# Expert lists made in pairs, and additions that skip places without a token

## The reference

```python
def hierarchical_moe(h, w_coarse, w_fine, w_up, w_down):
    coarse = softmax(t @ w_coarse)                   # 4 groups, the best one is taken
    fine = (t @ w_fine) of that group                # 4 experts, the best two are taken
    gates = softmax(top 2) * group probability       # zero for the other 14 experts
    gu = einsum('nd,edf->nef', t, w_up)              # 16 experts, 1024 -> 2 x 256
    act = silu(g_part) * u_part * gates
    out = einsum('nef,efd->nd', act, w_down)         # 256 -> 1024, summed over the experts
```

## Time and profile before

| | us |
|---|---|
| median of 3 runs (lowest, highest) | 625.59 (621.91, 627.24) |
| the profiled execution | 628.41 |
| its span | 626.7 |
| TensorE busy | 551.8 |
| VectorE busy | 375.3 |
| ScalarE busy | 262.8 |
| GpSimd busy | 191.5 |

### The profile page before, as it was taken

How to read it: one execution, slowest core, us unless ns; L and a number is a source line. 1 busy time by engine, 2 the same in 40 slices (tenths; PEclk the granted TensorE clock), 3 DMA queues, 4 the chain that set the end, 5 groups by cost and what they waited for, 6 DMA issues and landing times.

```text
span 626.7 us, 7175 instructions
## 1 busy us (share of the span) xinstructions
PE 551.8 (88%) x2589; PEld 432.6 (69%) x2589; DVE 375.3 (60%) x615; ACT 262.8 (42%) x421; POOL 191.5 (31%) x354
## 2 busy tenths in 40 slices
PE   1699799999979899989999789935799999999982
PEld 1488687887667677677888678835668677676750
DVE  3885176683983884956666632365865766665530
ACT  6415035435433545364223311131463666665631
POOL 2549333089469269000000000002021341313111
PEclk9999799988989989999999889965897999999997
DMA  8524520220220210113364561597479799999954
GB/s 302 107 69 110 160 66 2 68 67 2 68 67 2 67 51 1 52 51 100 98 208 158 208 253 68 200 396 276 126 262 347 243 376 340 372 341 371 345 96 69
DMA packets 69220, 102.82 MB, mean 164 GB/s; under 512 B 10528, under 2 KB 42304, under 8 KB 69184
## 3 DMA queue, kind: packets, MB, share of 16 engines
q1 hardware_dynamic: 63184, 80.84, 37.6%
q0 software_dynamic: 4608, 16.78, 10.7%
q10 hardware_dynamic: 1392, 4.74, 1.9%
HBM read 88.71 MB, written 12.58 MB: 162 GB/s over the span
## 4 chain that ended last, share of the span: by engine, by line
PE 61%; DVE 15%; DMA 7%; ACT 7%; POOL 4%; issue 3%; SPq 1%; ACTq 0%; POOLq 0%; DVEq 0%
PE pj L1477 8%; PE pj L1479 8%; PE pj L1478 8%; PE m L1794 7%; DMA arena_front<-in_w_expert_up_dram 4%; PE pj L1774 4%; PE pj L1775 4%; PE pj L1776 4%; PE sc L1554 2%; PE tp L1762 2%; ACT arena_back L755 1%; SPq L481 1%; DMA arena_front<-h_rows,idx_all 1%; DVE arena_back L1190 1%; ACT arena_back L764 1%
## 5 line engine op out<-in xcount | busy, mean ns | idle before, releaser
L1477 PE MATMUL pj<-h_high,split 128*128 128x512 f32 x192 | 81.3, 424 | 2.7 <-DVE h_low L963 1.5
L1478 PE MATMUL pj<-h_low,split 128*128 128x512 f32 x192 | 78.4, 409 | 0.0
L1479 PE MATMUL pj<-h_high,split 128*128 128x512 f32 x192 | 78.2, 407 | 0.0
L1411 DVE TENSOR_TENSOR up_low<-arena_front,up_high 128x2048 fp32r<-128x2048 f32 x26 | 59.2, 2290 | 21.9 <-ACT up_high L827 21.9
L1794 PE MATMUL m<-arena_back 128*128 128x512 f32 x128 | 58.3, 598 | 2.8 <-ACT arena_back L839 2.8
L605 POOL DMA_INDIRECT out_dram<-arena_back,idx_all x16 | 29.8, 1866 | 101.2 <-DMA out_dram<-arena_back,idx_all 87.4
L1774 PE MATMUL pj<-up_high,xt_high 128*128 128x512 f32 x128 | 56.1, 438 | 5.3 <-DVE up_low L1411 3.7
L519 POOL TENSOR_TENSOR rstd<-ssq,half_col 128x1 f32<-128x1 f32 x8 | 6.4, 796 | 166.2 <-DVE ssq L940 166.2
L827 ACT ACTIVATE up_high<-arena_front 128x2048 fp32r<-128x2048 f32 x26 | 49.5, 1916 | 6.6 <-DMA arena_front<-in_w_expert_up_dram 5.7
L1775 PE MATMUL pj<-up_low,xt_high 128*128 128x512 f32 x128 | 50.7, 396 | 0.0
L1776 PE MATMUL pj<-up_high,xt_low 128*128 128x512 f32 x128 | 50.7, 396 | 0.0
(11 more groups left out here) (316 smaller groups left out, 1241.4 us busy)
## 6 DMA issues: line engine op xcount, KB each, us to landing
arena_front<-in_w_expert_up_dram SPq DMA_DIRECT2D x13, 2048.0 KB, 15.9
arena_back<-in_w_expert_down_dram SPq DMA_DIRECT2D x16, 1024.0 KB, 12.8
arena_front<-in_w_in_dram SPq DMA_DIRECT2D x13, 1024.0 KB, 5.6
arena_back<-in_w_expert_up_dram SPq DMA_DIRECT2D x3, 2048.0 KB, 17.3
arena_front<-in_w_out_dram SPq DMA_DIRECT2D x4, 1024.0 KB, 5.3
arena_back<-in_x_dram SPq DMA_DIRECT2D x4, 512.0 KB, 5.9
arena_front<-in_w_ssm_glu_gate_dram SPq DMA_DIRECT2D x8, 256.0 KB, 2.8
arena_front<-in_w_ssm_glu_val_dram SPq DMA_DIRECT2D x8, 256.0 KB, 3.6
```

What stands on the lines that cost most here:

```text
L1411: tt(up_low[e % NU][:, half(h)], ring[e % NU][:, half(h)], up_high[e % 2][:, half(h)].bitcast(F32), ALU.subtract).then_inc(up_low_done, 1)
L1477: pe.matmul(dst, sh, mh, start=first and i == 0, stop=False)
L1478: pe.matmul(dst, sh, ml, start=False, stop=False)
L1479: ins = pe.matmul(dst, sl, mh, start=False, stop=last and i == len(terms) - 1)
```

## The change

The lists of the experts 8 to 15 become four sets of two. TensorE makes a pair behind the up product in steps 1 to 4. VectorE chooses the pair at the start of the same step and reads it at the start of the next. All sets but the second are in bank `sc[0]`, each at its own columns.

The fourth column of `tg` becomes the token's number for a routed token and the number plus 512 for another. VectorE reads it into a new tile, `idx_own`. The addition takes its rows from `idx_own` with a bound of 511: an index above the bound is left out, and is no error. Gathers go by `idx_all` as before, so a place without a routed token is still gathered, multiplied and scaled (by zero).

```diff
-    LISTS = [0, 2, NE // 2, NE]
+    LISTS = [0, 2] + list(range(NE // 2, NE + 1, 2))
...
+        idx_own = sb("idx_own", [P, NE], U32)
...
-                g.indirect_dma_start(out_rows, bass.IndirectOffsetOnAxis(idx_all[:, e:e + 1], 0), y_out[e % 2], None,
-                                     compute_op=ALU.add).then_inc(y_added, 16)
+                g.indirect_dma_start(out_rows, bass.IndirectOffsetOnAxis(idx_own[:, e:e + 1], 0), y_out[e % 2], None,
+                                     compute_op=ALU.add, bounds_check=SEQ - 1, oob_is_err=False).then_inc(y_added, 16)
...
-            for n in (0, 3):
-                mark(v.tensor_copy(tg[:, :, :, n], bc(tok_id[:, :].rearrange("p (o t) -> p o t", o=1), [P, NE, TT])))
+            mark(v.tensor_copy(tg[:, :, :, 0], bc(tok_id[:, :].rearrange("p (o t) -> p o t", o=1), [P, NE, TT])))
...
-            mark(ts(r(7), r(6), -1.0, 1.0, ALU.mult, ALU.add))
+            link(ts(r(7), r(6), -1.0, 1.0, ALU.mult, ALU.add))
+            mark(stt(tg[:, :, :, 3], ev(r(7)), float(SEQ), bc(tok_id[:].rearrange("p (o t) -> p o t", o=1), [P, NE, TT]),
+                     ALU.mult, ALU.add))
...
                 v.tensor_copy(idx_all[:, lo:hi], got[:, :, 0])
+                v.tensor_copy(idx_own[:, lo:hi], got[:, :, 3])
                 v.tensor_reduce(gate_all[:, lo:hi], got[:, :, 1:3], AX_X, ALU.add).then_inc(idx_done, 1)
...
             for e in range(NE):
-                if e == 3:
-                    fill_lists(2)
+                if 1 <= e <= LAST_LISTS:
+                    for n in range(LISTS[e + 1], LISTS[e + 2]):
+                        pick_list(n)
+                if 2 <= e <= LAST_LISTS + 1:
+                    read_lists(e)
                 if e + 1 < NE:
                     low_up(e + 1, 0)
...
                 up(e)
-                if e == 3:
-                    pe.wait_ge(idx_done, 2)
-                    place_lists(LISTS[2], NE)
+                if 1 <= e <= LAST_LISTS:
+                    pe.wait_ge(idx_done, e + 1)
+                    place_lists(LISTS[e + 1], LISTS[e + 2])
                 if e:
                     turn_act(e - 1)
```

More of the change, by code:

```diff
@@ L382, in split_low, with list_at @@
                               ).then_inc(low_done_p if n in on_pool else low_done_v, 1)
+        LAST_LISTS = len(LISTS) - 3
+        def list_at(k):
+            return 128 if k < 2 else 192 + 8 * k
         def half(h):
@@ L1381, in fill_lists, with pick_list, read_lists @@
             def fill_lists(k):
-                lo, hi = LISTS[k], LISTS[k + 1]
[L1384 to L1388, removed]
+                for e in range(LISTS[k], LISTS[k + 1]):
+                    pick_list(e)
+                read_lists(k)
+            def pick_list(e):
+                if e >= 2:
+                    v.wait_ge(idx_full, e - 1)
+                tt(pick[e % 2], bc(slot_no[:].rearrange("p (o n) -> p o n", o=1), [P, TT, CAP]),
+                   bc(pos[:, e, :].rearrange("p (t o) -> p t o", o=1), [P, TT, CAP]), ALU.is_equal).then_inc(pick_done, 1)
+            def read_lists(k):
+                lo, hi = LISTS[k], LISTS[k + 1]
                 v.wait_ge(idx_full, hi)
-                c0 = 128 + 64 * (k // 2)
-                got = sc[k % 2][:, c0:c0 + 4 * (hi - lo)].rearrange("p (e n) -> p e n", n=4)
+                c0 = list_at(k)
+                got = sc[int(k == 1)][:, c0:c0 + 4 * (hi - lo)].rearrange("p (e n) -> p e n", n=4)
                 v.tensor_copy(idx_all[:, lo:hi], got[:, :, 0])
+                v.tensor_copy(idx_own[:, lo:hi], got[:, :, 3])
                 v.tensor_reduce(gate_all[:, lo:hi], got[:, :, 1:3], AX_X, ALU.add).then_inc(idx_done, 1)
@@ L1749, in place_list @@
                 k = sum(e >= lo for lo in LISTS[1:])
-                c0 = 128 + 64 * (k // 2) + 4 * (e - LISTS[k])
+                c0 = list_at(k) + 4 * (e - LISTS[k])
                 pe.wait_ge(pick_done, e + 1)
                 for t in range(TT):
-                    ins = pe.matmul(sc[k % 2][:, c0:c0 + 4], pick[e % 2][:, t, :], tg[:, e, t, :], start=t == 0, stop=t == TT - 1)
+                    ins = pe.matmul(sc[int(k == 1)][:, c0:c0 + 4], pick[e % 2][:, t, :], tg[:, e, t, :], start=t == 0, stop=t == TT - 1)
                 ins.then_inc(idx_full, 1)
```

## The result

| | before | changed |
|---|---|---|
| median (16 runs each) | 626.83 us | 622.72 us |
| lowest, highest | 621.91, 632.18 | 618.34, 626.71 |
| ratio, 95% interval | | 0.9949, 0.9924 to 0.9973 |
| the profile's span | 626.7 us | 624.9 us |

The changed kernel is 0.5% faster, some 3.2 us, where 7.4 were forecast; the ratio compares fast executions with fast ones and is what the text goes by, while the two medians above are of all 16 and differ by 4.1 us. The gain is real (the interval does not reach 1) and the forecast of its size was wrong: the time lies between the forecast and rival 1's -1.8 us, nearer to the rival.

The account below looks back on a forecast made before the run. TensorE was taken to bound the kernel, weight loads just behind. TensorE -3.6, loads -1.15 and tail -2.6 gave -7.4 us, against a median of 625.6: 618.2 us, range 613 to 626 (likeliest case's own 614 to 621.5).

Parts of the forecast that it names:

- rival 1: Additions: engines serve fixed places, so some keep 8 rows; loads gain little, tail nothing; -1.8 us, 623.8 us, chance 0.24.
- What bounds the kernel: Expert steps: TensorE bounds at 10.02 us a step, the weight loads are a second limit just behind.
- The pairs: Steps 1 to 4: the 7.83 us stop in step 3 goes, four pairs at 0.95 us add 3.8.
- The index column: Before the first gather: one more linked operation and an extra read add 0.4 us, all on the path.
- The loads' lateness: Steps 10 to 14: 1.15 us late through an up-weight load; shorter additions would remove it, -1.15 us.
- The tail: Last two additions: first lands sooner, last issued 1.3 us sooner and 1.3 shorter; -2.6 us, ends 0 and -4.0.
- With half the rows, spread evenly: Additions under load: 1.35 us of engine time go from each step's 12.1; bounds nothing and 2.7.
- The 22.8% from 440 to 445: Software queue's share of 5 us, read as a gather of 128 rows: 1.14 us an engine, leaving 2.7 for an addition.
- Rival 2: Additions: the bound saves nothing, rows left out still pass as packets; 623.8 us, chance 0.10.
- the likeliest case: Whole kernel: TensorE, loads and tail all gain, -7.4 us to 618.2 us, chance 0.58; sign: packets down from 4608 by 1024.
- an estimate of 0.6 us for the last addition's gain: Last addition: by about 2.0 us plus bytes at 436 GB/s it loses 0.6 us, not 1.3; tail -1.9.

Follow-up runs that it names:

- e1: Changed kernel with the lists in pairs but all 128 rows added by idx_all, as before; ratio 0.9960 to the kernel before.
- e8: The changed kernel run again, nothing altered; ratio 0.9876 to the kernel before.
- e11: The changed kernel run a third time, nothing altered; ratio 0.9913 to the kernel before.
- e3: Changed kernel with place p holding rank p div 4 + 32 (p mod 4), spreading routed tokens; ratio 0.9869 to the kernel before.
- e5: Changed kernel with place p holding rank 2 (p mod 64) + p div 64; ratio 0.9873 to the kernel before.
- e10: The kernel of e3 run again, nothing altered; ratio 0.9805 to the kernel before.
- e4: Changed kernel with every row of every addition left out, experts' results missing from the output; ratio 0.9835 to the kernel before.

## Why the prediction was wrong

**What bounds the kernel**: right. TensorE's beat, with the loads just behind, and the loads did return as the bound when TensorE alone was sped up, now at step 13.

**The pairs**: right, and better than the sum by 0.7 us. Put at -7.83 + 3.8 = -4.0 us, measured -4.7 up to step 4 (e1: -4.9 to step 5). A pair costs 10.87 - 10.02 = 0.85 us and not 0.95. No pair waited. On VectorE the added work went into idle time as said; in step 2 of the changed kernel, idle before in brackets:

```profile
462.42 1.29 DVE L1399 TENSOR_TENSOR pick<-slot_no,pos 128x512 fp32r<-128x512 f32 x2
463.63 0.15 DVE L1408 CAST idx_all<-sc 128x2 uint32<-128x2 f32 x1
463.70 0.15 DVE L1409 CAST idx_own<-sc 128x2 uint32<-128x2 f32 x1
463.76 0.15 DVE L1410 TENSOR_REDUCE gate_all<-sc 128x2 f32<-128x4 f32 x1
463.83 2.28 DVE L1428 TENSOR_TENSOR up_low<-arena_front,up_high 128x2048 fp32r<-128x2048 f32 x1
466.67 2.29 DVE L1428 TENSOR_TENSOR up_low<-arena_front,up_high 128x2048 fp32r<-128x2048 f32 x1 [0.55 <-ACT up_high L834]
```

The idle time before the second half fell from 1.66 to 0.55 us.

**The index column**: as put in this pair of traces, but not shown. From the router's product at L1721 (411.74) to the first gather (429.91) there are 18.17 us; in the kernel before, L1701 starts at 410.25 and the gather at 428.02, 17.77. +0.40. The same stretch of the same code is 18.33 us in e8 and 17.29 in e11, so that it came out at just +0.40 is in part luck.

**The loads' lateness**, -1.15: wrong, it grew to 1.9, so +0.75. **The tail**, -2.6: wrong. From the end of step 14 to the program's end there were 26.5 us and are 26.7: +0.2. Both terms rest on one step, and that is the one that failed: "With half the rows, spread evenly". The rows were counted per list, rightly, and then divided by 16. The engine with the most rows decides when an addition has landed, and its number of rows had not changed. With the rows spread (e3, e5, e10) both terms came as put: no lateness in any of the three, and 24.0 to 24.1 us from the end of step 14 to the end, 2.4 to 2.5 less than before where 2.6 were worked out. The whole was 0.987, 0.987 and 0.981 for a forecast of 0.988.

One reading behind the terms was wrong without harm. The 22.8% from 440 to 445 were taken for a gather of 128 rows, but its 0.43 MB are only 105, so a gather costs an engine nearer 1.4 us than 1.14, and an addition under load nearer 2.5 than 2.7.

The sum with what was measured: -4.7 + 0.4 + 0.75 + 0.2 = -3.35 us, against -3.2 by the ratio.

**Rival 1** was right in its mechanism. Its -1.8 us was too small by 1.4: the pairs gave 0.7 more than put, and the loads came sooner than by the 1.8 us that it allowed. The load of the last expert's weights landed 163.3 us after the first gather before, and 158.2 in the changed kernel; that of expert 14, which now is the late one, 150.8 and 149.4. In e1, where all rows are added, the last one landed at 158.0, so the rows left out are not the reason; what is, no run shows. **Rival 2** was right that each place left out remains a packet, and wrong that it costs: the prediction's own sign for the likeliest case, 1024 packets fewer, was a wrong sign. The chance of rival 1, 0.24, was too low. Nothing in the rows spoke for an even split, and the one statement at hand on the order of engines, which the prediction cites, spoke against it.

The Trainium skill ("DMA: Bandwidth & Descriptors", Anatomy of one DMA) gave an estimate of 0.6 us for the last addition's gain with even rows. The runs e3 and e5 show 6.3 us from issue to end where the changed kernel and e11 have 7.5 and 7.7, so 1.2 to 1.4: here the traces and that formula differ, and the last addition's gain is nearer to the 1.3 us worked out from rows on the fullest engine.

## What to carry to other kernels

Here an addition of an undisturbed tail landed 5.9 to 6.3 us after its issue as long as some engines kept eight rows, and 4.5 to 4.8 us with the same rows spread, three to five on each. So leaving out work helps only if the fullest engine loses some: ask which items are left out, and by which engine each was carried. With a list of 128 places through GpSimd, fill the places in an order that visits all engines (place p holding rank p div 4 + 32 (p mod 4)); here it costs one changed iota and gives 4.6 us more in the trace, where the whole change gave 3.7. Before crediting a saving to a shared resource, look whether its share can fall without its users gaining: a share below full beside a user that waits (0.75 and 0.68 in two of the three waits here) is a sign of it, though it was full in the third.

## What the runs showed of the hardware

- A row left out by the bound still makes a packet and costs next to nothing: with 128 of them the last addition lands 2.7 us after its issue where one with 128 rows takes 6.3 (e4, before).
- A row addition of 4 KB costs an engine 0.42 us alone, a gathered row 1.14 x 16 / 105 = 0.17 us: two to three times as much, which the byte counts don't show.
- Places 0 to 63 of a 128-row addition are carried by one half of the engines and 64 to 127 by the other, four neighbouring places at a time; the first 32 places of each half already reach all of its engines (e3, e5, e6).
- The best complete version measured is the changed kernel with its places spread: 0.9869 and 0.9805 of the time before in e3 and e10, and 0.9873 with the halves of e5.
